# Forgetting attention: probabilities and values split in two, three fp32r passes for one fp32 product

## The chip, the cores and the metric

One core of one Trainium2 chip (trn2) runs the whole program. The metric is the device time of one execution, in microseconds (us). Three runs of the kernel before gave 3176.74, 3176.81 and 3177.16 us; their median is 3176.81. The clock of TensorE has two levels, 1.2 and 2.4 GHz; the profile gives the granted share of the upper one.

## The reference, cut to what matters

A decoder trunk of two layers over 1024 tokens of width 1024: a retention layer and a forgetting-attention layer, each with an MLP. The attention has 16 heads of width 64 and reads keys, values and a cumulative forget gate `f`:

```
logits = q k^T * scale + f[query] - f[key]      (causal, query block against all keys before it)
p = softmax(logits)                             per query row
y = p @ v                                       then sigmoid(og) * y, then @ w_out
```

All is fp32, and the kernel keeps about fp32 precision on TensorE, which has a fast format, fp32r (a rounded fp32), and a slow one, full fp32.

## The kernel before, in words

Projections and the MLP split each operand into a rounded fp32r part ("high") and the rest ("low") and add three fp32r products; ScalarE rounds (`prep`, L646, into `w_hi`), VectorE subtracts (L988, into `w_lo`).

In attention, queries and keys are split the same way and stacked, high and low, on 128 partitions, together with the forget gate in `a2`, `b2`. Probabilities and values are not: `values` (L1887) is a full fp32 product.

For each head `h` of the loop at L1913, TensorE does three things, interleaved by block `n` of twelve (`fox_blocks`: key block against up to 512 queries; in order, 512, 384, 256, 128, 512, 512, 128, 512, 256, 512, 384, 512 columns, 4608 in all):

- `logits(h, n + 1)`: keys by queries, two fp32r passes (L1881, L1882) and for blocks on the diagonal a mask (L1884), into one of two banks;
- `score_tile(h + 1, t)`, queries by keys, for the row maxima of the **next** head (L1857, L1859): eight tiles of 1024 down to 128 columns, in two alternating pairs of banks. A tile waits until the tile two before it was read. `tiles_at` says at which block each stands: at blocks 0 to 6, in heads 0 and 8 at blocks 3 to 8;
- `values(h, n)`: 64 value columns and 64 columns of ones by the probabilities of block `n` (L1902), so that the sum of the probabilities comes out beside the result. It waits for the exponential.

ScalarE takes the exponential of each block of logits (`exps`, L932) into `probs`, and the reciprocal of the sums as Ln and Exp (`inverse_sum`, L941, L943). `z_high` (L949) rounds the gated result of a pair of heads for the out projection.

VectorE takes the maximum of each score tile (`row_max`, L1372), splits the eight columns of maxima in two (`split_max`, L1379, L1381); TensorE transposes them (`max_transpose`, L1868), VectorE copies the rows (`copy_max`, L1385), SP writes them by two DMAs into `a2` of the next head (`save_max`, L435), and `logits(h + 1, 0)` waits for those. VectorE also multiplies the result by the reciprocal and by the gate (`y_gate`, L1395, L1399) and takes the low part of a pair (`z_low`, L1405).

GpSimd issues all other loads of the stage: eight DMAs of queries, keys and gates for head `h + 3` (`load_qk`, L589) once the logits of head `h` are done, the values (`load_v`, L595), the output gate of a pair (`load_og`, L598). Its only arithmetic is the sum of squares before a norm (L502). A first head has places of its own in memory (`q_first` and so on).

After heads 7 and 15 follows the out projection of eight heads (L1517, L1520, L1521), which reads `z_hi`, `z_lo` pair by pair.

Of the kernel before, what the change touches and what calls it, by code (L numbers as in the profile page):

```python
# [21 lines left out]
ALU = mybir.AluOpType  # L22
# [7 lines left out]
P = 128  # L30
# [67 lines left out]
def build(nc, x, vec_a, vec_b, forget_bias, positions, w_ada, kv_w_ada, w_mlp_in, w_mlp_out, ret_w_in,  # L98
          ret_w_out, kv_w, fox_w_in, fox_w_out, ret_decay, out):
    with ExitStack() as ctx:  # L100
# [18 lines left out]
        ((h_hi, h_lo), (rq, rk, rv, rg, rdec, qdec, rs, k_tok, qd), (q1, k1, q2, k2, fv, fog, row_mask), (out_stage,),  # L119
# [7 lines left out]
             ("fv", [P, 2, 8, P], F32), ("fog", [P, S], F32), ("row_mask", [P, S], BF16)],  # L127
# [3 lines left out]
            _, rq_first, rk_first, rv_first) = region(  # L131
# [6 lines left out]
             ("rv_first", [P, 4, RET_DV], F32)])  # L138
# [3 lines left out]
        (misc,), (q1_first, k1_first) = region(  # L142
            20 * 1024, [("misc", [P, 5, S], F32)], [("q1_first", [P, S], F32R), ("k1_first", [P, S], F32R)])
        low_tiles = sb("low_tiles", [P, 2, S])
# [31 lines left out]
        probs = misc[:, 0:4, :].rearrange("p a (b n) -> p (a b) n", n=HALF)  # L176
        y_fox = misc[:, 4, :]
        fv_first = stage[:, 4, :].rearrange("p (b n) -> p b n", n=P)
        qk_hi = misc[:, 3:5, :].bitcast(F32R)
        log_sum = low_tiles[:, 0, :].rearrange("p (b n) -> p b n", n=HALF)  # L180
        max_rows = low_tiles[0:16, 1, 0:P]
# [39 lines left out]
        def scratch(name, shape):  # L221
# [50 lines left out]
        fox_v_loaded = [sem(f"fox_v_loaded{i}") for i in range(2)]  # L272
        first_qk_loaded, first_v_loaded, first_ones_set, second_qk_loaded = (
            sem("first_qk_loaded"), sem("first_v_loaded"), sem("first_ones_set"), sem("second_qk_loaded"))
# [4 lines left out]
        st_full, exp_done, pv_done = sem("st_full"), sem("exp_done"), sem("pv_done")  # L279
        log_done, inv_done, y_read, y_gated = sem("log_done"), sem("inv_done"), sem("y_read"), sem("y_gated")  # L280
        ones_set, row_mask_set = sem("ones_set"), sem("row_mask_set")
# [30 lines left out]
        def probs_slot(e):  # L312

            return 4 + e % 4 if e < NF else e % 8

        def probs_before(e):

            return e - 4 if e < NF + 4 else e - 8

        def tiles_at(h, n):  # L320

            places = {3: (0,), 4: (1,), 5: (2,), 6: (3,), 7: (4, 5), 8: (6, 7)} if h % 8 == 0 else \
                {0: (0,), 1: (1,), 2: (2,), 3: (3,), 4: (4,), 5: (5,), 6: (6, 7)}
            return places.get(n, ())

        def transpose_at(h):

            return 10 if h % 8 == 0 else 8
# [23 lines left out]
        def _(sp):  # L352
# [74 lines left out]
            with sp.Fori(0, 4) as i:  # L427
                for j in range(2):
                    load_pair(i * 2 + (W_FQ + j), j, in_pair(fox_w_in, i * 512 + 256 * j))
            def save_max(h):  # L430

                sp.wait_ge(s_read, h * 9 + 9)
                for n in range(2):
                    row = fox_tiles(h)[2][68 + n:69 + n, :].bitcast(F32)
                    sp.dma_start(row, max_rows[8 * n:8 * n + 8, :]).then_inc(max_loaded, 16)  # L435
            for g in range(2):
                for j in range(2):
                    load_pair(g * 2 + (W_FOX + j), j, out_pair(fox_w_out, g * 512, j))
                for h in range(9) if g == 0 else range(9, FOX_HEADS):
                    save_max(h)  # L440
                    if h == 0:
                        sp.wait_ge(a_full, A_MLP1)
                        for dst, src in head_parts(1)[:4]:
                            sp.dma_start(dst, src).then_inc(second_qk_loaded, 16)
            mlp_loads(W_MLP1, 1)
# [10 lines left out]
        def _(pool):  # L456
# [129 lines left out]
            def load_qk(h, done, first=0):  # L586

                for dst, src in head_parts(h)[first:]:
                    pool.dma_start(dst, src).then_inc(done, 16)  # L589

            def load_v(h):
                at = h % 2 * 64
                rows = fv_s.rearrange("(b p) n -> p b n", p=P)[:, :, h * 64:h * 64 + 64]
                dst, done = (fv_first, first_v_loaded) if h == 0 else (fv[:, h % 2], fox_v_loaded[h % 2])
                pool.dma_start(dst[:, :, at:at + 64], rows).then_inc(done, 16)  # L595

            def load_og(pr):
                pool.dma_start(fog[:], og_s[pr]).then_inc(og_loaded, 16)  # L598
# [8 lines left out]
            load_qk(0, first_qk_loaded)  # L607
            load_v(0)
            with pool.Fori(0, 2) as i:
                for j in range(4):  # L610
                    spill(j, og_s[bass.ds(i * 4 + j, 1)].rearrange("a p n -> p (a n)"),
                          a_free, i * 4 + (A_OG + j + 1))
            pool.wait_ge(a_full, A_MLP1)
            load_qk(1, fox_qk_loaded[1], 4)
            for j in range(4):
                pool.wait_ge(stage_dma[j], E_OG + 32)
            load_og(0)
            load_v(1)
            load_qk(2, fox_qk_loaded[2])
            load_v(2)  # L620
            load_qk(3, fox_qk_loaded[0])
            for h in range(FOX_HEADS):
                if h and h + 3 < FOX_HEADS:
                    wait_run(st_full, h * NF + NF)
                    load_qk(h + 3, fox_qk_loaded[h % 3])
                if h and h + 2 < FOX_HEADS:
                    wait_run(pv_done, h * NF + NF)
                    load_v(h + 2)
                if h % 2 and h + 1 < FOX_HEADS:
                    wait_run(y_gated, h * 2 + 2)  # L630
                    load_og(h // 2 + 1)
# [4 lines left out]
        def _(act):  # L636
# [289 lines left out]
            def exps(h, n):  # L926
# [3 lines left out]
                if probs_before(e) >= 0:  # L930
                    act.wait_ge(pv_done, probs_before(e) + 1)
                nc.scalar.activation(probs[:, probs_slot(e), 0:w], bank[4 + e % 2][:, 0:w], ACT.Exp).then_inc(exp_done, 1)  # L932

            def inverse_sum(h, n):
# [7 lines left out]
                act.wait_ge(log_done, v + 1)  # L942
                nc.scalar.activation(log_sum[sums, n, :], log_sum[sums, n, :], ACT.Exp, scale=-1.0).then_inc(inv_done, 1)  # L943

            def z_high(pr, n):

                cols = slice(HALF * n, HALF * (n + 1))
                act.wait_ge(y_gated, pr * 4 + n + 3)
                nc.scalar.activation(z_hi[:, pr % 4, cols], y_fox[:, cols], ACT.Copy).then_inc(z_hi_done, 1)  # L949
            for h in range(FOX_HEADS):  # L950
                for n in range(NF):
                    exps(h, n)
                    if n == 0 and h % 8:
                        inverse_sum(h - 1, 1)
                    if n in (4, 5) and h % 2 == 0 and h % 8:
                        z_high(h // 2 - 1, n - 4)
                    if n == 6:
                        inverse_sum(h, 0)
                if h % 8 == 7:
                    g = h // 8  # L960
                    inverse_sum(h, 1)
                    z_high(h // 2, 0)
# [13 lines left out]
        def _(dve):  # L976
# [410 lines left out]
            def y_gate(h, n):  # L1387
# [3 lines left out]
                v = h * 2 + n  # L1391
                dve.wait_ge(inv_done, v + 1)
# [3 lines left out]
                if h % 2 == 0 and n == 0:  # L1396
                    dve.wait_ge(og_loaded, h * 8 + 16)
                dve.wait_ge(y_read, v + 1)
                TT(y_fox[mine, cols], y_fox[mine, cols], fog[mine, cols], ALU.mult).then_inc(y_gated, 1)  # L1399
# [9 lines left out]
            nc.vector.memset(fv_first[:, :, 64:128], 1.0).then_inc(first_ones_set, 1)  # L1409
# [10 lines left out]
            nc.vector.memset(fv[:, 1, :, 0:64], 1.0).then_inc(ones_set, 1)  # L1420
            nc.vector.memset(fv[:, 0, :, 64:128], 1.0).then_inc(ones_set, 1)
# [4 lines left out]
            def next_max(h, tiles):  # L1426
                if h + 1 < FOX_HEADS:
                    for t in tiles:
                        row_max(h + 1, t)
            for h in range(FOX_HEADS):  # L1430
                if h % 8 == 0:
                    next_max(h, (0, 1))
                    y_gate(h, 0)
                    next_max(h, (2, 3, 4, 5, 6, 7))
                else:
                    next_max(h, (0, 1))
                    y_gate(h - 1, 1)
                    next_max(h, (2, 3, 4))
                    if h % 2 == 0:
# [553 lines left out]
```

## Time and profile before

| | |
|---|---|
| Median of 3 runs | 3176.81 us |
| The profiled execution's own time | 3181.35 us |
| Its span, first to last instruction | 3179.8 us |
| Mean granted clock of TensorE | 0.991 |
| Busy share of the span: TensorE, VectorE, ScalarE, GpSimd | 98%, 41%, 27%, 7% |
| Attention heads 0 to 7, then 8 to 15 | 2062 to 2223 us, 2267 to 2417 us |

The busy time is that of records whose ends are modelled for TensorE, so what a pass costs is read from the start of one to the start of the next. GpSimd's busy time has its DMA issues in it where they show.

### The profile page before, as it was taken

To read this page: it belongs to the slowest core of one execution; us is meant where nothing else is said; L and a number is where in the kernel's file an instruction comes from. 1 tells how busy PE (TensorE), PEld (TensorE's weight loads), DVE (VectorE), ACT (ScalarE), POOL (GpSimd) and SP (SyncE) were. 2 spreads that over 40 slices of the span, in tenths; PEclk is the share of its full clock that TensorE was granted. 3 is DMA by queue.
4 is the path that set the end of the run, shared out by engine and by line. 5 is a ranking of instruction groups with operands and counts; after the bars stand their busy time and mean duration, and the time that the engine had idled before them with its cause. 6 is when DMAs were issued, how large, how long until landed. Compare 5 with 4: busy or idle time off the path is not lost.

```text
span 3179.8 us, 34523 instructions
## 1 busy us (share of the span) xinstructions
PE 3121.0 (98%) x13726; PEld 2491.4 (78%) x13726; DVE 1308.1 (41%) x1542; ACT 859.3 (27%) x1025; POOL 222.8 (7%) x343
## 2 busy tenths in 40 slices
PE   7999999999999999999999999989999999999999
PEld 4788888877778888888887777756767788888887
DVE  5664323255555333333353243145454533333323
ACT  4111222222242111111134344234244211111112
POOL 0000010000010000000010001023021000000000
PEclk8999999999999999999999999999999999999999
DMA  5555565433201111111112324255241111111111
GB/s 219 189 191 199 176 221 203 174 111 110 97 27 40 53 53 42 50 53 40 54 40 104 109 87 155 96 126 125 65 109 50 40 53 53 40 53 53 40 53 54
DMA packets 144652, 302.50 MB, mean 95 GB/s; under 512 B 10241, under 2 KB 72116, under 8 KB 144564
## 3 DMA queue, kind: packets, MB, share of 16 engines
q1 hardware_dynamic: 111204, 185.90, 17.8%
q0 software_dynamic: 33360, 115.38, 11.7%
q8 instruction: 61, 1.00, 0.1%
q14 instruction: 27, 0.22, 0.0%
HBM read 245.93 MB, written 55.18 MB: 95 GB/s over the span
## 4 chain that ended last, share of the span: by engine, by line
PE 91%; DVE 4%; ACT 2%; DMA 2%; issue 1%; POOL 0%; SPq 0%; DVEq 0%; ACTq 0%; POOLq 0%
PE ps L1521 10%; PE ps L1517 10%; PE ps L1520 10%; PE ps L1478 8%; PE ps L1481 8%; PE ps L1484 8%; PE ps L1634 5%; PE ps L1640 5%; PE ps L1637 5%; PE ps L1902 3%; PE ps L1608 3%; PE ps L1611 3%; PE ps L1612 3%; PE ps L1758 1%; PE ps L1730 1%; PE ps L1857 1%
## 5 line engine op out<-in xcount | busy, mean ns | idle before, releaser
L1517 PE MATMUL ps<-z_hi,w_hi 128*128 128x512 f32 x1408 | 552.0, 392 | 0.0
L1521 PE MATMUL ps<-z_hi,w_lo 128*128 128x512 f32 x1408 | 548.0, 389 | 0.0
L1520 PE MATMUL ps<-z_lo,w_hi 128*128 128x512 f32 x1408 | 547.8, 389 | 0.0
L1478 PE MATMUL ps<-h_hi,w_hi 128*128 128x512 f32 x1152 | 452.0, 392 | 3.9 <-DVE w_lo L988 3.9
L1481 PE MATMUL ps<-h_lo,w_hi 128*128 128x512 f32 x1152 | 449.0, 390 | 0.0
L1146 DVE SCALAR_TENSOR_TENSOR xT<-ps,ada,xT 128x512 f32<-128x512 f32 x352 | 258.8, 749 | 443.3 <-PE ps L1521 443.3
L646 ACT ACTIVATE w_hi<-w_raw 128x2048 fp32r<-128x2048 f32 x116 | 221.4, 1909 | 738.7 <-PE ps L1517 487.7
L988 DVE TENSOR_TENSOR w_lo<-w_raw,w_hi 128x2048 fp32r<-128x2048 f32 x116 | 265.7, 2290 | 246.1 <-ACT w_hi L646 246.1
L1484 PE MATMUL ps<-h_hi,w_lo 128*128 128x512 f32 x1152 | 355.1, 389 | 0.0
L1634 PE MATMUL ps<-h_hi,w_hi 128*128 128x512 f32 x768 | 305.1, 397 | 9.1 <-DVE xT L1146 5.5
L1520 PEld LDWEIGHTS ps<-z_lo,w_hi 128*128 128x128 f32 x1408 | 264.3, 188 | 56.7 <-issue 2.2
L1517 PEld LDWEIGHTS ps<-z_hi,w_hi 128*128 128x128 f32 x1408 | 264.3, 188 | 56.6 <-issue 2.2
L1521 PEld LDWEIGHTS ps<-z_hi,w_lo 128*128 128x128 f32 x1408 | 264.3, 188 | 55.1
L1637 PE MATMUL ps<-h_hi,w_lo 128*128 128x512 f32 x768 | 302.1, 393 | 0.0
L1298 DVE TENSOR_TENSOR misc<-misc 128x1024 f32<-128x1024 f32 x64 | 78.3, 1223 | 452.9 <-ACT misc L834 452.9
L1478 PEld LDWEIGHTS ps<-h_hi,w_hi 128*128 128x128 f32 x1152 | 216.7, 188 | 50.7 <-DVE w_lo L988 3.5
L1481 PEld LDWEIGHTS ps<-h_lo,w_hi 128*128 128x128 f32 x1152 | 216.7, 188 | 45.8 <-issue 1.2
L1484 PEld LDWEIGHTS ps<-h_hi,w_lo 128*128 128x128 f32 x1152 | 216.5, 188 | 45.4
L1640 PE MATMUL ps<-h_lo,w_hi 128*128 128x512 f32 x768 | 251.7, 394 | 0.4 <-DVE h_lo L1030 0.4
L834 ACT ACTIVATE misc<-ps 128x1024 f32<-128x1024 f32 x64 | 65.8, 1028 | 498.8 <-PE ps L1484 250.8
L1634 PEld LDWEIGHTS ps<-h_hi,w_hi 128*128 128x128 f32 x768 | 146.3, 190 | 42.8 <-DVE xT L1146 6.3
L1640 PEld LDWEIGHTS ps<-h_lo,w_hi 128*128 128x128 f32 x768 | 146.3, 190 | 32.3 <-DVE h_lo L1030 1.4
(261 smaller groups left out, 3612.2 us busy)
## 6 DMA issues: line engine op xcount, KB each, us to landing
misc<-w_ada SPq DMA_DIRECT2D x80, 512.0 KB, 5.1
w_raw<-w_mlp_in SPq DMA_DIRECT2D x32, 1024.0 KB, 5.5
w_raw<-w_mlp_out SPq DMA_DIRECT2D x32, 1024.0 KB, 5.0
w_raw<-ret_w_in SPq DMA_DIRECT2D x24, 1024.0 KB, 7.8
qk_s<-stage POOLq DMA_DIRECT2D x16, 512.0 KB, 4.0
v_s<-stage POOLq DMA_DIRECT2D x16, 512.0 KB, 3.6
g_s<-stage POOLq DMA_DIRECT2D x16, 512.0 KB, 3.9
misc<-kv_w_ada SPq DMA_DIRECT2D x16, 512.0 KB, 5.5
```

The costliest lines, as they stand in the source:

```text
L646: nc.scalar.activation(w_hi[:, slot, :], w_raw[:, slot, :], ACT.Copy).then_inc(hi_done, 1)
L988: TT(w_lo[:, slot, :], w_raw[:, slot, :], w_hi[:, slot, :].bitcast(F32), ALU.subtract)\
L1146: STT(out=x_half, in0=bank[ring[q % 4]], scalar=ada[:, gate + q % 8:gate + q % 8 + 1], in1=x_half, op0=ALU.mult, op1=ALU.add).then_inc(d_f ...
L1478: m = MM(outs[hf], hi, b_hi[:, k, cols], start=first, stop=False)
L1481: MM(outs[hf], hi, b_lo[:, k, cols], start=False, stop=False)
L1484: m = MM(outs[hf], lo, b_hi[:, k, cols], start=False, stop=last)
L1517: mm = MM(out_bank, hi, z_hi[:, k, half(hf)], start=k == 0, stop=False)
L1520: MM(out_bank, hi, z_lo[:, k, half(hf)], start=False, stop=False)
L1521: mm = MM(out_bank, lo, z_hi[:, k, half(hf)], start=False, stop=k == 3)
L1634: m = MM(outs[u][hf], w[u][0], h_hi[:, k, half(hf)], start=k == 0, stop=False)
L1637: MM(outs[u][hf], w[u][1], h_hi[:, k, half(hf)], start=False, stop=False)
L1640: m = MM(outs[u][hf], w[u][0], h_lo[:, k, half(hf)], start=False, stop=k == KT - 1)
```

## The change

Probabilities and values are each split into a rounded part and a rest, and `values` becomes three fp32r passes: high values by high probabilities, low by high, high by low.

- Probabilities. ScalarE takes the exponential twice, once into the fp32r tile `probs_hi` and once into `probs`; for blocks 7, 9 and 11 VectorE copies `probs` to `probs_hi` in place of the first. The rest, `probs - probs_hi`, goes to `probs_lo`: on VectorE for blocks 5, 7, 9, 11 (and for the whole of head 0), on GpSimd for the others. `probs_hi` and `probs_lo` lie in slot 1 of `w_hi` and `w_lo`. Each of the tiles has four slots (before, `probs` had eight).
- Values. GpSimd loads them raw, copies them to fp32r (`v_high`) and subtracts (`v_low`); the low parts have zeros where the high ones have the ones.
- TensorE's order: `logits(n + 1)`, score tiles, the two high passes of block `n`, the low pass of block `n - 1`, then the transpose, now at block 7 (in heads 0 and 8 still 10). The low pass of block 11 stands behind the next head's first logits.
- `load_qk` and `load_og` move from GpSimd's queue to SP's, behind `save_max`, for head `h + 2`.
- `y_gate` is parted: `y_scale` for each head, `gate` for a pair of heads at once on 128 partitions. `inverse_sum` is parted in two on ScalarE.
- VectorE's order is written out block by block.

The diff, cut to its core:

```diff
-            return 10 if h % 8 == 0 else 8
+            return 10 if h % 8 == 0 else 7
...
+        HI_ON_DVE = (7, 9, 11)
+        LO_ON_DVE = (5, 7, 9, 11)
+        def low_part(engine, h, n):
+            e, w = h * NF + n, fox_blocks[n][3]
+            engine.wait_ge(exp_done, e + 1)
+            engine.wait_ge(*hi_ready(e))
+            if e >= 4:
+                engine.wait_ge(pv_done, e - 3)
+            engine.tensor_tensor(probs_lo[:, e % 4, 0:w], probs[:, e % 4, 0:w], probs_hi[:, e % 4, 0:w].bitcast(F32),
+                                 ALU.subtract).then_inc(lo_ready(e)[0], 1)
...
 SP, for each head
+                    elif h + 2 < FOX_HEADS:
+                        if h > 1:
+                            sp.wait_ge(st_full, h * NF)
+                        load_qk(h + 2, fox_qk_loaded[(h + 2) % 3])
+                    if h and h % 2 == 0:
+                        sp.wait_ge(y_gated, h)
+                        load_og(h // 2)
...
 GpSimd
-            for h in range(FOX_HEADS):
-                if h and h + 3 < FOX_HEADS:
-                    wait_run(st_full, h * NF + NF)
-                    load_qk(h + 3, fox_qk_loaded[h % 3])
...
+            for h in range(1, FOX_HEADS):
+                for n in (0, 1, 2, 3):
+                    low_part(nc.gpsimd, h, n)
+                if h + 1 < FOX_HEADS:
+                    v_high(h + 1)
+                low_part(nc.gpsimd, h, 4)
+                if h + 1 < FOX_HEADS:
+                    v_low(h + 1)
+                for n in (6, 8, 10):
+                    low_part(nc.gpsimd, h, n)
+                if h + 2 < FOX_HEADS:
                     load_v(h + 2)
...
 ScalarE, exps
+                if e >= 4:
+                    act.wait_ge(*lo_ready(e - 4))
+                if not hi_on_dve(e):
+                    if e >= 4:
+                        act.wait_ge(pv_hi_done, e - 3)
+                    nc.scalar.activation(probs_hi[:, e % 4, 0:w], bank[4 + e % 2][:, 0:w], ACT.Exp).then_inc(p_hi_act, 1)
+                nc.scalar.activation(probs[:, e % 4, 0:w], bank[4 + e % 2][:, 0:w], ACT.Exp).then_inc(exp_done, 1)
...
 VectorE
+            def high_part(h, n):
+                e, w = h * NF + n, fox_blocks[n][3]
+                dve.wait_ge(exp_done, e + 1)
+                if e >= 4:
+                    dve.wait_ge(pv_hi_done, e - 3)
+                    dve.wait_ge(*lo_ready(e - 4))
+                nc.vector.tensor_copy(probs_hi[:, e % 4, 0:w], probs[:, e % 4, 0:w]).then_inc(p_hi_dve, 1)
...
+                for n in range(NF):
+                    if hi_on_dve(h * NF + n):
+                        high_part(h, n)
+                    if lo_on_dve(h * NF + n):
+                        low_part(nc.vector, h, n)
+                    if h + 1 < FOX_HEADS:
+                        for t in tiles_at(h, n):
+                            row_max(h + 1, t)
+                        if n == (8 if h % 8 == 0 else 6):
+                            split_max(h + 1)
+                        if n == transpose_at(h):
+                            copy_max(h + 1)
+                    if h % 8 and n == 1:
+                        y_scale(h - 1, 1)
+                        if h % 2 == 0:
+                            gate(h // 2 - 1, 1)
+                    if h % 2 == 0 and h % 8 and n in (4, 6):
+                        z_low(h // 2 - 1, n // 2 - 2)
+                    if n == 8:
+                        y_scale(h, 0)
+                        if h % 2:
+                            gate(h // 2, 0)
...
 TensorE
-                MM(bank[6 + hf][:, HALF - w:HALF], keys, probs[:, probs_slot(e), 0:w],
-                   start=b == 0, stop=n in (HF0 - 1, NF - 1)).then_inc(pv_done, 1)
+                dst = bank[6 + hf][:, HALF - w:HALF]
+                MM(dst, high[:, b, :], probs_hi[:, e % 4, 0:w], start=b == 0, stop=False)
+                MM(dst, low[:, b, :], probs_hi[:, e % 4, 0:w], start=False, stop=False).then_inc(pv_hi_done, 1)
+            def values_low(h, n):
+                pe.wait_ge(*lo_ready(e))
+                MM(bank[6 + hf][:, HALF - w:HALF], fox_values(h)[0][:, b, :], probs_lo[:, e % 4, 0:w], start=False,
+                   stop=n in (HF0 - 1, NF - 1)).then_inc(pv_done, 1)
...
                 logits(h, 0)
+                if h % 8:
+                    values_low(h - 1, NF - 1)
                 for n in range(NF):
                     if n + 1 < NF:
                         logits(h, n + 1)
                     if h + 1 < FOX_HEADS:
                         for t in tiles_at(h, n):
                             score_tile(h + 1, t)
-                    values(h, n)
+                    values_high(h, n)
+                    if n:
+                        values_low(h, n - 1)
```

## Rows read from the trace of the kernel before

**Rows 1.** The page, the chain that ended last, by engine.

```profile
PE 91%; DVE 4%; ACT 2%; DMA 2%; issue 1%; POOL 0%; SPq 0%; DVEq 0%; ACTq 0%; POOLq 0%
```

**Rows 2.** Stretches: us, PE, PEld, DVE, ACT, POOL busy (x count), clock, DMA.

```profile
2080.00:2100.00 20.00, 15.41 (x60) 9.58 (x59) 7.03 (x20) 5.82 (x11) 1.25 (x3) 0.91 0.55 114
...
2280.00:2300.00 20.00, 16.73 (x60) 10.81 (x61) 6.57 (x18) 4.97 (x10) 5.06 (x9) 0.83 0.45 95
```

**Rows 3.** The transpose of the maxima (L1868), its starts in steady heads.

```profile
L1868 PE MATMUL ps<-ident,max_split x7: 277/277/278, 2109.7 to 2218.9; 128*16 128x128 f32 x7
```

**Rows 4.** Stretches: two steady heads, and head 15.

```profile
2164.38:2200.68 36.30, 36.20 (x162) 23.93 (x162) 20.39 (x48) 17.28 (x34) 10.61 (x19) 1.00 0.54 119
2401.74:2416.80 15.06, 14.35 (x59) 8.46 (x57) 2.75 (x4) 8.00 (x16) 0.00 (x0) 1.00 0.21 65
```

**Rows 5.** Order of time in a steady head: start us, us, engine, line.

```profile
2161.75 0.28 PE L1857 MATMUL ps<-k,q 128*128 128x256 f32 x1
...
2161.95 0.60 ACT L932 ACTIVATE misc<-ps 128x512 f32<-128x512 f32 x1 [0.18 <-PE ps L1882]
...
2162.05 0.27 PE L1859 MATMUL ps<-k,q 68*128 68x128 f32 x1
2162.16 0.43 PE L1902 MATMUL ps<-misc,fv 128*128 128x128 f32 x2
...
2162.74 1.08 PE L1902 MATMUL ps<-misc,fv 128*128 128x512 f32 x2
...
2163.90 0.39 PE L1882 MATMUL ps<-q,k 70*128 70x512 f32 x1
...
2164.16 0.17 DVE L1381 TENSOR_TENSOR max_split<-neg_max,max_split 128x8 f32<-128x8 f32 x1
...
2164.38 0.28 PE L1868 MATMUL ps<-ident,max_split 128*16 128x128 f32 x1
```

**Rows 6.** Order of time in the out projection, two passes of 512.

```profile
2264.02 0.39 PE L1517 MATMUL ps<-z_hi,w_hi 128*128 128x512 f32 x1
...
2264.25 0.39 PE L1520 MATMUL ps<-z_lo,w_hi 128*128 128x512 f32 x1
```

**Rows 7.** Groups by form: busy us, mean ns of one, idle before.

```profile
L932 ACT ACTIVATE misc<-ps 128x512 f32<-128x512 f32 x96 | 57.3, 597 | 117.2 <-PE ps L1882 59.9 <-PE ps L1884 57.2
...
L1405 DVE TENSOR_TENSOR z_lo<-misc,z_hi 128x512 fp32r<-128x512 f32 x16 | 10.4, 686 | 0.1
...
L1379 DVE CAST max_split<-neg_max 128x8 fp32r<-128x8 f32 x16 | 2.7, 171 | 0.6
...
L1061 DVE CAST misc<-misc 128x1024 f32<-128x1024 int32 x1 | 0.7, 694 | 10.2 <-DMA misc<-positions 10.2
```

**Rows 8.** Order of time in the norm after attention, VectorE and GpSimd.

```profile
2456.03 2.28 DVE L988 TENSOR_TENSOR w_lo<-w_raw,w_hi 128x2048 fp32r<-128x2048 f32 x1
2456.49 2.97 POOL L502 TENSOR_TENSOR low_tiles<-misc 128x512 f32<-128x512 f32 x1 [20.00 <-ACT misc L653]
...
2458.89 1.12 DVE L1023 SCALAR_TENSOR_TENSOR misc<-xT,mod,low_tiles 128x512 f32<-128x512 f32 x1
```

**Rows 9.** GpSimd's sums of squares (L502): ns min/median/max.

```profile
L502 POOL TENSOR_TENSOR low_tiles<-low_tiles,misc x24: 1283/1298/1569, 923.4 to 2465.1; 128x512 f32<-128x512 f32 x24
```

**Rows 10.** Order of time: waits in heads 0, 1, 5 and 9.

```profile
2065.28 1.12 PE L1902 MATMUL ps<-misc,stage 128*128 128x512 f32 x2 [2.01 <-ACT misc L932]
...
2088.89 1.40 SPq L435 DMA_DIRECT2D q<-low_tiles  x2
...
2094.03 0.50 PE L1881 MATMUL ps<-q,k 128*128 128x512 f32 x1 [3.78 <-DMA q<-low_tiles]
...
2165.00 1.30 SPq L435 DMA_DIRECT2D q<-low_tiles  x2
...
2168.22 0.79 PE L1881 MATMUL ps<-q,k 128*128 128x512 f32 x1
...
2289.65 0.79 PE L1881 MATMUL ps<-q,k 128*128 128x512 f32 x1 [3.27 <-DMA q<-low_tiles]
```

More of the change, by code:

```diff
@@ L584, in _, with v_tile, v_high, v_low @@
             spill_heads(fq_hi_s, fq_lo_s, 8)
-            def load_qk(h, done, first=0):
-                for dst, src in head_parts(h)[first:]:
-                    pool.dma_start(dst, src).then_inc(done, 16)
+            def v_tile(h):
+                return v_raw_first if h == 0 else v_raw[:]
             def load_v(h):
-                at = h % 2 * 64
[L593 to L598, printed above, removed]
+                if h > 1:
+                    pool.wait_ge(v_split_done, h)
+                rows = fv_s.rearrange("(b p) n -> p b n", p=P)[:, :, h * 64:h * 64 + 64]
+                pool.dma_start(v_tile(h), rows).then_inc(v_raw_loaded, 16)
+            def v_high(h):
+                at = h % 2 * 64
+                pool.wait_ge(v_raw_loaded, 16 * (h + 1))
+                if h >= 2:
+                    pool.wait_ge(pv_done, (h - 1) * NF)
+                nc.gpsimd.tensor_copy(fox_values(h)[0][:, :, at:at + 64], v_tile(h)).then_inc(v_hi_done, 1)
+            def v_low(h):
+                at = h % 2 * 64
+                high, low = fox_values(h)
+                pool.wait_ge(v_hi_done, h + 1)
+                if h == 1:
+                    pool.wait_ge(zeros_set, 1)
+                if h == 2:
+                    pool.wait_ge(zeros_set, 2)
+                nc.gpsimd.tensor_tensor(low[:, :, at:at + 64], v_tile(h), high[:, :, at:at + 64].bitcast(F32),
+                                        ALU.subtract).then_inc(v_split_done, 1)
             for j in range(4):
@@ L947, in z_high @@
                 cols = slice(HALF * n, HALF * (n + 1))
[L948 removed]
+                act.wait_ge(y_gated, pr * 2 + n + 1)
                 nc.scalar.activation(z_hi[:, pr % 4, cols], y_fox[:, cols], ACT.Copy).then_inc(z_hi_done, 1)
@@ L1424, in _ @@
             dve.wait_ge(row_mask_set, 2)
[L1426 to L1429, printed above, removed]
             for h in range(FOX_HEADS):
[L1431 to L1439, printed above, removed]
-                        z_low(h // 2 - 1, 0)
-                        z_low(h // 2 - 1, 1)
-                    next_max(h, (5,))
-                    y_gate(h, 0)
-                    next_max(h, (6, 7))
-                if h + 1 < FOX_HEADS:
-                    split_max(h + 1)
-                    copy_max(h + 1)
+                if h == 1:
+                    dve.wait_ge(st_full, NF)
+                    nc.vector.memset(fv_low_even[:, :, 64:128].bitcast(F32), 0.0).then_inc(zeros_set, 1)
+                for n in range(NF):
[20 more added lines that the diff above has]
+                            gate(h // 2, 0)
                 if h % 8 == 7:
                     g = h // 8
-                    y_gate(h, 1)
+                    y_scale(h, 1)
+                    gate(h // 2, 1)
                     z_low(h // 2, 0)
```

158 lines of the change are left out of this document (96 added, 62 removed).

## The prediction

> **What bounds the kernel now.** I read the page's chain first: TensorE holds 91% of it [rows 1]. Only one stage changes, the sixteen attention heads (the loop at L1913, 2062 to 2417 us), so the rest was read there. The table by stretches shows a granted clock of 0.91 and 0.83 around the starts of heads 1 and 9, each after a wait [rows 2]. The transpose of the maxima runs once a head and paces it: seven of them from 2109.7 to 2218.9, 109.2 / 6 = 18.2 us apart [rows 3]. Over two such heads (36.3 us) TensorE is busy for 36.2, VectorE for 20.4, ScalarE for 17.3, GpSimd for 10.6 (all DMA issues) [rows 4]. So in 13 steady heads (1 to 7, 9 to 14) TensorE's own work is the bound. Heads 0 and 8 end in a wait for the row of maxima; head 15 has no score tiles.
>
> **TensorE's part.** In the order of time, the values of a block of 512 and the first logits pass after them take 2162.74 to 2163.90, 1.16 us [rows 5]. A pass of 512 in fp32r starts 0.23 after the one before it (2264.02, 2264.25 [rows 6]). So one block of 512 of fp32 values costs 0.92. A head has 4608 columns of them: six blocks of 512, two each of 384, 256 and 128. Before, in proportion: 6 x 0.92 + 2 x (0.69 + 0.46 + 0.23) = 8.3 us. After, three passes a block: 18 x 0.23 = 4.1, and 6 x (0.18 + 0.12 + 0.10) = 2.4, since narrow passes cost more than their columns (a pass of 128 takes 0.11, from 2162.05 to 2162.16 [rows 5]): 6.5. That takes 1.8 us a head off TensorE. The transpose's wait for VectorE, 0.25 (2163.90 + 0.23 to 2164.38), is covered by other work after. 18.2 - 1.8 - 0.25 = 16.1.
> On the page "FP8 and Floating Point Precision" (TensorE Precision Notes) the Trainium skill has true FP32 as four passes. By that alone a quarter of 8.3, 2.1 us a head, would go, not 1.8; rows 5 bear out the four.
>
> **What is added.** ScalarE: a second exponential, into `probs_hi`, for nine of twelve blocks: 3 x 0.60 + 2 x (0.49 + 0.38 + 0.28) = 4.1 us (L932; 384 and 256 in proportion [rows 7]). From 8.6 us a head [rows 4] to 12.7. VectorE: four subtractions of 512 at 0.69, as L1405, and three copies of 512. No row shows such a copy; its bounds are 0.17 (L1379, 8 columns) and 0.69 (L1061, 1024 columns) [rows 7]; in proportion, 0.43. That is 4.1 us. Gating a pair at once gives back 0.7. From 10.2 to 13.6, and some 0.04 a hand-off. GpSimd: subtractions of 2560 columns; L502 takes 1.28 us at 512 [rows 9], so 6.4, plus `v_low` 1.3 and `v_high` (0.5 to 1.3; 0.7, nearer a copy than a subtraction). It loses eight DMA issues, which go to SP, where two row transfers a head stand. Behind SP's new waits (`st_full`, `y_gated`) stand loads with most of a head to spare and the next `save_max`, whose data come later than both. No engine's sum reaches 16.1, so the order of the waits decides.
>
> **The chain in the second half of a head.** TensorE to ScalarE takes 0.20 (the next pass takes over at 2161.75, the exponential starts at 2161.95), VectorE to TensorE 0.05 (2164.16 + 0.17 to 2164.38) [rows 5]; I take 0.05 from ScalarE too. By hand, in program order, with these durations: up to block 5 TensorE waits only in even heads, 0.3, for maximum 2 behind `gate`; GpSimd's low parts come 0.7 to 1.2 us early. Then:
> (a) Score tile 7 needs maximum 5, which stands behind `low_part` 5 on VectorE. Begun at once, nothing waits.
> (b) High pass 7 needs maximum 7 (0.45), the split (0.35), in even heads `z_low` (0.69), and copy 7 (0.43): 0.7 us odd, 1.0 even.
> (c) High pass 9 needs copy 9, behind `copy_max`, `y_scale` and in odd heads `gate` (0.28 + 0.69 + 0.69): 0.9 odd, 0.4 even.
> (d) High pass 11 needs exponential 11 (0.60), copy 11 (0.43) and hand-offs, 1.3 us; TensorE has 0.55 of work beside it: 0.75.
> Odd 2.35, even 2.45: with 16.1 that is 18.5. The 2 us saved come back as waits for VectorE.
>
> **The shared resource.** In the norm after attention, GpSimd's L502 began at 2456.49 inside VectorE's L988, which ended at 2458.31, and took 2.97 us: 1.15 after L988's end. VectorE's L1023 of 2458.89 took 1.12, to 0.55 after that GpSimd op's end at 2459.46 [rows 8]. So ops of the two with both inputs in SBUF exclude each other. In the changed head, GpSimd runs `low_part` 4 and `v_low`, 2.6 us in a row, just when `low_part` 5 comes up on VectorE, by my walk 0.2 us after `v_low` began. Blocked, it is 1.1 late: (a) becomes 0.75 in odd heads and, with `z_low` caught too, 1.3 in even ones, so the head takes 19.5. The order hangs on 0.2 us, less than my walk can tell, so I take the middle, 19.0. Thirteen heads: 13 x (19.0 - 18.2) = +10.4. Bounds: -27 (16.1, no wait) and +23 (20.0, the later ones caught too).
> By the Trainium skill, "SBUF — State Buffer", section "SBUF: two separate sides", the port pair is an exclusive lock for the whole instruction, against VectorE ops with two SBUF inputs and its 2-port modes. Rows 8 agree for the first; for copies no row shows it. By that rule the sum would be the second rival's.
>
> **The edges.** Head 1's logits wait 3.8 us for the row of maxima, issued at 2088.89 and there at 2094.03, 5.1 us, while GpSimd's loads for heads 2 and 3 are under way; in a steady head 3.2 is enough (2165.00 to 2168.22). Head 9's wait 3.3, with eight loads issued beside the row [rows 10]. After, those loads stand behind the row on SP: 1.9 and 1.3 less. The wait falls below 2 us, like the one of 2.0 at 2065.28, after which passes kept their length [rows 10], so the half clock goes too: 0.91 and 0.83 over 20 us are 3.6 and 6.8 us at the lower of its two levels, 1.8 and 3.3 us lost [rows 2]. Head 0's own saving goes to VectorE, which has all its subtractions: 0; head 8 saves about 1. So -3.7 and -5.6; bounds of both together 0 (another wait in its place) and -13. Head 15: 15.1 us now [rows 4]; after, ScalarE's 11.5 with (c) and (d): 13.3, -1.8. At the ends of heads 7 and 15 the added low pass waits 0.1, and projection steps of three other pairs cover the rest: 0. The first head's split and the memsets lie under its DMA wait: 0, or 1 us if not. Edges: -11.1.
>
> **Sum.** +10.4 - 11.1 = -0.7 against this execution's own 3181.35 us; the median of the runs lies 4.5 lower: 3176.8 - 0.7, 3176 in round figures. A measurement of this kernel can tell about 0.2% from no change, 6.4 us.
>
> **Rivals.**
> *TensorE stays the bound.* The walk may be slow: back-to-back ops start 0.1 before the one ahead ends, and half of (b) to (d) would go: 17.3 us a head, 13 x -0.9 - 11.1 = -23, 3154; without any wait 3139. For it: VectorE's sum leaves 2.5 us free. Against: (d) is a bare chain. Chance 0.30.
> *The lock decides* (slower): at `low_part` 5, `z_low` and copies and subtractions 7 to 11, against GpSimd's 4, 6, 8, 10 and `v_low`. Beyond 19.0 us a head the change loses; at 19.5 to 20.2 it is +17 to +26 less 11.1: 3183 to 3192, middle 3188. For it: rows 8. Against: GpSimd's late ops are narrow. Chance 0.20.
> *The row waits anyway*: SP late, or slowed as before; both heads stay at half clock, +8, 3184. Chance 0.06.
> *Passes don't get cheap*: three weight loads a block don't hide, the 1.8 us are not saved: +10 or more, 3190. The projection's passes, each with its load at 0.23 [rows 6], speak against. Chance 0.06.
>
> **How the numbers follow.** The likeliest, waits for VectorE that eat the saving, has 0.38, range 3166 to 3186: 0.09 below 3170.4, 0.25 within, 0.04 above 3183.2. Faster 0.30 + 0.09 = 0.39. Same 0.25 + 0.02 (lock) + 0.03 (row) + 0.01 (passes) = 0.31. Slower 0.04 + 0.18 + 0.03 + 0.05 = 0.30. The range 3148 to 3200 reaches past half-gone waits and takes in the lock with edges that pay only half.
>
> **What would show it.** Passes of values 0.23 apart; transposes 18.5 to 19.5 us apart; TensorE's waits put down to VectorE's copies (blocks 7, 9, 11) and to the maximum of tile 5; subtractions on VectorE above 1 us beside GpSimd's; clock 1.00 after heads 0 and 8. Transposes below 17.5 apart, or waits put down to GpSimd's low parts, would prove the walk wrong.

## The result, and the profile after

The changed kernel takes 3208.99 us (median of 4 runs, 3206.89 to 3210.04), the kernel before 3176.98 us beside it (3176.74 to 3179.32): a ratio of 1.0097, 95% interval [1.0084, 1.0110]. It is slower by 32 us. The forecast of 3176 missed, and so did its range, which ended at 3200.

The profiled executions span 3208.5 us after and 3179.8 us before, so the 28.7 us between them are what the traces can place. The transpose of the maxima (now L1974) paces the heads as before [rows 3]. Its starts in the order of time on TensorE (start, us, engine, line):

```profile
2151.05 0.27 PE L1974 MATMUL ps<-ident,max_split 128*16 128x128 f32 x1
...
2172.64 0.41 PE L1974 MATMUL ps<-ident,max_split 128*16 128x128 f32 x1
...
2192.03 0.27 PE L1974 MATMUL ps<-ident,max_split 128*16 128x128 f32 x1
...
2213.64 0.41 PE L1974 MATMUL ps<-ident,max_split 128*16 128x128 f32 x1
```

They are 21.6, 19.4 and 21.6 us apart, where they were 18.2 apart. I call the step that holds blocks 0 to 7 of head h (and blocks 8 to 11 of the head before it) "head h": odd heads take 19.4, even ones 21.6 (heads 2 and 3, 21.1 and 19.2). The 28.7 us divide so (after less before; a transpose has the number of the head whose maxima it turns): the first transpose comes 0.9 later; step 0 to 1, +2.9; 1 to 2, -2.8; the six steps 2 to 8, +13.0; 8 to 9, +3.1; 9 to 10, -2.5; the five steps 10 to 15, +12.6; from there to the end, +1.5. The eleven steady steps make +25.6, nearly all of it. Four of the other terms also hold a moved block: the transpose stands one block earlier than before, but not in heads 0 and 8, so the steps 1 to 2 and 9 to 10 hold one block less than before, and 8 to 9 and the stretch behind the last transpose one more. Such a block (number 8) takes 1.0 us in after (2151.05 to 2152.10), and 1.9 at the lower clock behind the last transpose.

Stretches of after (us, busy of PE, PEld, DVE, ACT, POOL, clock, DMA): heads 2 and 3, heads 5 and 6, four microseconds in each of heads 2 and 6 around block 7, and the starts of heads 1 and 9, to set beside [rows 2, 4]:

```profile
2110.74:2151.05 40.31, 35.16 (x189) 27.58 (x188) 29.70 (x61) 23.25 (x52) 20.71 (x23) 1.00 0.49 108
2172.64:2213.64 41.00, 36.43 (x188) 28.74 (x187) 29.44 (x60) 23.25 (x52) 20.70 (x22) 0.96 0.48 105
...
2130.00:2134.00 4.00, 2.77 (x16) 2.11 (x15) 3.70 (x9) 1.73 (x5) 0.74 (x1) 1.00 0.01 1
2212.00:2216.00 4.00, 3.48 (x12) 2.84 (x12) 2.89 (x6) 0.83 (x2) 0.74 (x1) 0.57 0.01 1
...
2080.00:2100.00 20.00, 16.88 (x72) 12.17 (x71) 11.90 (x30) 8.23 (x18) 2.28 (x2) 0.83 0.45 97
2300.00:2320.00 20.00, 17.77 (x80) 13.61 (x79) 11.04 (x22) 8.96 (x20) 8.90 (x10) 0.83 0.42 95
```

TensorE is no longer its own bound: 36.4 us busy of 41.0, with a clock of 0.96, where it had 36.2 of 36.3 [rows 4]. No other engine is full either (VectorE 29.4). So the order of waits decides. The largest waits of TensorE in the heads, 2040 to 2460 us (line, waited for: us in total, times, longest):

```profile
PE ps L2011 <- DVE w_hi L1497: 28.4, 41, 1.1
PE ps L1963 <- DVE neg_max L1459: 6.3, 13, 0.8
PE ps L1963 <- DMA k<-fk_hi_s: 6.2, 1, 6.2
PE ps L2011 <- ACT w_hi L1008: 3.1, 4, 2.0
PE ps L1987 <- DMA q<-mean_head: 2.6, 2, 1.3
```

L2011 is the high pass, L1497 the copy that rounds the probabilities of blocks 7, 9 and 11 on VectorE: 41 waits of about 0.7 us. L1963 is a score tile, L1459 the row maximum that frees its buffer. An even head shows how they come about (order of time: start, us, engine, line, [idle before <- released by]):

```profile
2206.99 1.29 POOL L669 TENSOR_TENSOR fv_low_odd<-v_raw,fv 128x512 fp32r<-128x512 f32 x1
...
2207.53 1.29 DVE L1503 TENSOR_TENSOR z_lo<-misc,z_hi 128x512 fp32r<-128x512 f32 x1
...
2208.75 0.94 DVE L346 TENSOR_TENSOR w_lo<-misc,w_hi 128x512 fp32r<-128x512 f32 x1
...
2210.28 0.33 PE L1963 MATMUL ps<-k,q 128*128 128x128 f32 x1 [0.78 <-DVE neg_max L1459]
...
2212.04 0.42 DVE L1497 CAST w_hi<-misc 128x512 fp32r<-128x512 f32 x1
...
2212.51 0.80 PE L2011 MATMUL ps<-w_hi,fv 128*128 128x512 f32 x1 [0.98 <-DVE w_hi L1497]
2213.11 0.63 PE L2012 MATMUL ps<-w_hi,fv_low_even 128*128 128x512 f32 x1
2213.54 0.31 PE L2019 MATMUL ps<-w_lo,fv 128*128 128x128 f32 x1
```

While GpSimd subtracts (L669, `v_low`), VectorE's `z_low` takes 1.29 us for its 0.69, `low_part` 5 comes late behind it, so maximum 5, and tile 7 waits 0.78 for that. Then the high pass of block 7 waits 0.98 for its copy. `low_part` 5 takes 1.61 to 1.62 in the odd heads, where `v_low` catches it itself, and copy 11 0.62 us for its 0.43 (0.77 in head 2): it begins while GpSimd issues the load of the next values (L650, 0.91 us from 2155.10) and ends 0.22 after that (2155.61 to 2156.23). Behind the two waits of this even head the granted clock is 0.57: L2012 starts 0.60 after L2011 and L2019 0.43 after that, in place of 0.34 and 0.24 in head 2. The passes are as slow up to 2215.6, so the next step runs slow as well. The even heads 4, 6, 10, 12 and 14 all have such a stretch, of 0.66 over 5 us behind block 7. Head 2 has not: the same two waits, 0.76 and 0.98 us, stand in it at 2128.98 and 2131.21, and the clock stayed at 1.00.

### The profile page after: what moved, and what is told of

Read it like the earlier page. It is cut to its first block and busy times, and to the rows that moved or that the text cites. A ratio compares the mean times of both kernels' runs of the same rounds, so it can differ in the third digit from the quotient of the medians.

```text
span 3208.5 us, 35519 instructions
## 1 busy us (share of the span) xinstructions
PE 3117.1 (97%) x13918; PEld 2525.7 (79%) x13918; DVE 1381.8 (43%) x1649; ACT 907.0 (28%) x1169; POOL 302.6 (9%) x371
```

## The experiments

Each kernel was timed beside the kernel before. Three theories stood against one another at the start. **L**: the exclusion of the two-input operations of GpSimd and VectorE makes the loss. **Q**: VectorE's own queue is enough. **C**: the half clock in even heads is part of it, and follows its waits. "Odd" and "even" are us of a steady head by the starts of the transposes, as most of them take it (head 7 of e3 took 20.6, head 4 of e8 18.4). "Copies" are the three of blocks 7, 9 and 11 on VectorE.

| | edit to the changed kernel | us, median | ratio to before, interval | odd | even |
|---|---|---|---|---|---|
| before | | 3177 to 3179 | | 18.1 | 18.3 |
| after | none | 3209.0 | 1.0097 [1.0084, 1.0110] | 19.4 | 21.6 |
| e1 | `v_low` late | 3193.8 | 1.0052 [1.0035, 1.0069] | 18.9 | 20.3 |
| e2 | `z_low` late | 3198.7 | 1.0064 [1.0047, 1.0081] | 19.7 | 19.7 |
| e3 | both late | 3208.4 | 1.0094 [1.0077, 1.0111] | 22.1 | 19.5 |
| e4 | before, loads on SP | 3173.8 | 0.9987 [0.9978, 0.9997] | 18.1 | 18.3 |
| e5 | no copies | 3173.2 | 0.9981 [0.9972, 0.9991] | 17.4 | 18.2 |
| e6 | no copies, `v_low` late | 3164.6 | 0.9958 [0.9941, 0.9974] | 17.2 | 17.6 |
| e7 | no low parts | 3185.3 | 1.0026 [1.0016, 1.0036] | 18.3 | 19.6 |
| e8 | no copies, low parts all on VectorE | 3179.9 | 1.0006 [0.9997, 1.0016] | 18.1 | 19.4 |
| e9 | no low parts, no copies | 3157.7 | 0.9938 [0.9921, 0.9954] | 17.1 | 17.1 |
| e10 | e6, head 1's loads from two queues | 3165.7 | 0.9964 [0.9952, 0.9975] | 17.1 | 17.6 |
| e11 | no low parts on GpSimd | 3187.7 | 1.0029 [1.0016, 1.0042] | 18.3 | 19.8 |
| e12 | e3 without copies | 3165.3 | 0.9963 [0.9949, 0.9977] | 17.5 | 17.5 |

**e1, the split of the values late.**

```diff
-                if h + 1 < FOX_HEADS:
-                    v_high(h + 1)
-                low_part(nc.gpsimd, h, 4)
-                if h + 1 < FOX_HEADS:
-                    v_low(h + 1)
-                for n in (6, 8, 10):
+                for n in (4, 6, 8, 10):
                     low_part(nc.gpsimd, h, n)
+                if h + 1 < FOX_HEADS:
+                    v_high(h + 1)
+                    v_low(h + 1)
```

> The changed kernel with one move: GpSimd's v_high and v_low for the next head stand behind its low_part 10 instead of around low_part 4. Theory L (the exclusion of two-input operations of GpSimd and VectorE makes the loss): in the changed kernel low_part 5 on VectorE took 1.61 us beside v_low and z_low 1.29; both go back to 0.69, tile 7 no longer waits, heads with odd numbers go from 19.4 to about 18.7 us, heads with even ones from 21.6 to 19.5 to 20.5, the whole about 12 to 18 us faster than the changed kernel (3192 to 3197). Theory Q (the order on VectorE alone, with z_low, split and copy 7 in a row): the waits move by less than 0.3 us a head, gain under 4 us.

15 us came back, the clock is 1.00 in two steady heads (2165 to 2204), and even heads fell by 1.3. So the collision in the middle of the head costs, and the half clock goes with it. The collision itself only moved: `v_low` now stands beside `low_part` 11, which takes 1.60 us, and TensorE waits 0.25 a head for that, where tile 7 had waited 0.78 in even heads and 0.24 in odd ones.

**e2, z_low late**: called at `n in (8, 10)` in place of `(4, 6)`.

> The changed kernel with one move: VectorE's two z_low of a pair stand at blocks 8 and 10 instead of 4 and 6. Theory Q: only even heads change, the copy of block 7 comes 1.3 us earlier, the wait that ends in half clock (21.6 us against 19.4) goes, even heads reach about 19.5: 6 heads x 2.1 = 12 us faster than the changed kernel, 3196. Theory L: low_part 5 is still caught by v_low, even heads stay above 20, gain 5 to 8 us. [...]

10 us came back and all heads take the same 19.7, with clock 1.00. That is nearer to Q (3196) than to L (3201 to 3204, with even heads above 20), though `low_part` 5 is still caught (1.61 and 1.28 us). High pass 7 of even heads waits 0.41 for its copy where it waited 0.98. Odd heads have no `z_low`, but the transpose cuts a head at block 7, so the work moved to blocks 8 and 10 lies in the step of the next, odd head; that took 0.3 more and the even one 1.9 less.

**e3, both.**

> The changed kernel with both moves. Theory L and Q together: odd heads 18.7, even heads 18.7, clock 1.00 in all steady heads; 13 heads x 18.7 against 7 x 19.4 + 6 x 21.6 = 265.4, so 22 us faster than the changed kernel: 3187, still 10 us slower than the kernel before, because of the waits for the copies of blocks 9 and 11. If the waits at copies 9 and 11 grow by what is saved ahead of them, only 10 us are gained.

Nothing came back, though each alone had, and neither of the figures expected for it (3187, or 10 us gained) was met. The trace of e3 shows why, in the second half of an even head, which lies in the step of the next, odd one:

```profile
2129.81 1.09 DVE L1501 TENSOR_TENSOR z_lo<-misc,z_hi 128x512 fp32r<-128x512 f32 x1
...
2130.44 1.58 POOL L669 TENSOR_TENSOR fv_low_odd<-v_raw,fv 128x512 fp32r<-128x512 f32 x1
2130.83 1.48 DVE L1495 CAST w_hi<-misc 128x512 fp32r<-128x512 f32 x1
...
2132.36 0.50 PE L2009 MATMUL ps<-w_hi,fv 128*128 128x512 f32 x1 [1.91 <-DVE w_hi L1495]
```

With `z_low` on VectorE at blocks 8 and 10 and `v_low` on GpSimd in the same place, copy 11 falls into `v_low`: it takes 1.48 us for its 0.43 and ends 0.29 after it. TensorE waits 1.91, and its clock from 2132 to 2136 is 0.67. One collision was taken away and another made.

**e4, the edges alone.** The kernel before with its DMA issues for queries, keys and gates moved to SP as in the change; values stay on GpSimd, probabilities in fp32.

> The kernel before with one part of the change: the loads of queries, keys and the output gate go from GpSimd's queue to SP's, behind the row of maxima; probabilities and values stay fp32. My step on the edges: head 9 and head 1 get their row in 3.2 us after its issue and keep the full clock, 4 to 9 us faster than before, 3168 to 3173. Rival: head 1's first score tile waits longer for its keys, since SP issues them one after another at 0.6 us (in the changed kernel that wait was 6.2 us against 4.0): 1 to 3 us of it are given back, 3172 to 3176.

By its starts the step 1 to 2 fell from 21.4 to 17.2 and 9 to 10 from 22.4 to 17.2 (-4.2 and -5.2; the prediction had -3.7 and -5.6), with clock 1.00 in both places. But step 0 to 1 grew by 3.5: head 1's first tile waits 7.9 us for its keys where it waited 4.0. With 3173.8 the rival's range (3172 to 3176) holds, and mine (3168 to 3173) just does not. The trace is of the fastest of the ten executions, 3169.2, so the clock of 1.00 in both places may not be in all of them.

**e5 and e6, no copies.** The same edit of one line in both, e6 with that of e1 as well:

```diff
-        HI_ON_DVE = (7, 9, 11)
+        HI_ON_DVE = ()
```

> The rounded probabilities of blocks 7, 9 and 11 of each head are written by a second exponential on ScalarE (as for the other nine blocks) and not by a copy on VectorE. In the trace of after, TensorE waits 28.4 us in all (41 times) for that copy. ScalarE is busy for 11.6 us of an average head, so three more exponentials of 0.60 us fit. Theory L (the exclusion of the two-input operations of GpSimd and VectorE makes those copies late; with no copy only blocks 9 and 11's rounded part is in time, and what is left is the third pass and the tile's maximum): the waits of the second kind go and odd heads fall from 19.4 us to about 17.4, even ones from 21.6 to about 18.5: 3209 - 14 x 2.5 = about 3174. Theory Q (VectorE's queue as a whole is the bound, 14.8 us of operations a head plus what they wait for one another): only the 1.3 us a head of the copies comes back, and the waits move to the low parts and the maxima: 3209 - 18 = about 3190.

> As the last one, and GpSimd splits the next head's values after its last low part, as in e1_vlow_late (which gave 3194 where after gave 3209). Theory L: with no copy on VectorE at block 11, the late split of the values has only row maxima and low part 11 to hold up, so the gain of both adds: odd and even heads near 17.4 us, about 3168. Theory Q: 3186 to 3190, as the last. If the late split delays low part 11 (third pass of block 11, then the next head's first), heads stay at 18 to 18.5: about 3180.

e5 gives back 36 us and e6 44, by which e6 beats both kernels: 13 us under before. The waits for VectorE's copies are gone. In e5 the largest that is left in steady heads is the one collision that theory L names, in even heads:

```profile
2193.31 1.73 POOL L669 TENSOR_TENSOR fv_low_odd<-v_raw,fv 128x512 fp32r<-128x512 f32 x1
...
2193.82 1.77 DVE L346 TENSOR_TENSOR w_lo<-misc,w_hi 128x512 fp32r<-128x512 f32 x1
...
2196.18 0.33 PE L1963 MATMUL ps<-k,q 128*128 128x128 f32 x1 [1.25 <-DVE neg_max L1459]
```

e6 takes it away too. The waits of TensorE in e6 from 2100 to 2220, nearly seven heads, are these three and no more:

```profile
PE ps L2017 <- POOL w_lo L346: 0.4, 1, 0.4
PE ps L2017 <- DVE w_lo L346: 0.3, 1, 0.3
PE ps L2009 <- ACT w_hi L1006: 0.2, 1, 0.2
```

e5 met L's figure (3174); Q's 3190 for it is out. e6 came 3 us under its own (3168). But L's reason, that the exclusion makes the copies late, is not what e5 shows: e7, next, has the same waits for copies without any of them stretched. The figure was right by luck.

**e7 and e9, no low parts.** The third pass reads the rounded part; e7 keeps the copies, e9 does not.

> Left out: every low part of the probabilities, on both engines; the third pass reads the rounded part instead, so that TensorE still runs its three passes; buffers are released by the values' end. It tells what TensorE's own work of a head comes to when no subtraction stands beside it. The prediction had 16.1 us a head for it (18.2 before). If that was right, heads come at 16.1 to 16.5 us, but for what the copies of blocks 7, 9 and 11 cost: theory L expects nearly nothing of them without the exclusion (16.5 to 17.0 a head, about 3209 - 14 x 3.8 = 3156). If the three passes are not as cheap as three plain ones (theory P), heads come at over 17.3 with hardly a wait on TensorE: 3165 or more.

> Left out: every low part of the probabilities (the third pass reads the rounded part, as in e7_no_low_parts), and the rounded parts of blocks 7, 9 and 11 are written on ScalarE. So neither copies nor subtractions stand on VectorE, and TensorE should be its own bound: this measures the term of the prediction that had 16.1 us a head. Theory R (the term was right): 16.1 to 16.3 us a head, even and odd alike. Theory M (mis-sized: the rows of e6 give 6.97 us a head for the three passes where the prediction took 6.5): 16.5 to 16.9 a head, about 3157 less than e6's 17.1 to 17.9 allow: 3150 to 3158.

e7 missed by 29 us. Without a single low part, on either engine, heads still take 18.3 and 19.6: each of its three copies a head takes 0.43 and none was stretched, but TensorE waits 28.2 us in all for them (46 times), as much as in after. The copies cost by their place in VectorE's queue, with no help of the exclusion; theory P, which had hardly a wait on TensorE, is out as well. e9 then gives TensorE's own work: 17.1 a head, even and odd alike, where the prediction had 16.1. Its time, 3157.7, is at the upper end of what theory M gave (3150 to 3158), its heads are above M's 16.5 to 16.9. Its passes, in the order of time on TensorE:

```profile
2156.49 0.23 PE L1979 MATMUL ps<-ident_b,mask_b 128*128 128x128 bf16 x1
2156.53 0.42 PE L2000 MATMUL ps<-w_hi,fv 128*128 128x384 f32 x1
2156.79 0.34 PE L2001 MATMUL ps<-w_hi,fv_low_even 128*128 128x384 f32 x1
2156.97 0.39 PE L2008 MATMUL ps<-w_hi,fv 128*128 128x512 f32 x1
2157.41 0.50 PE L2000 MATMUL ps<-w_hi,fv 128*128 128x512 f32 x1
```

A pass of 384 takes 0.18 (2156.79 to 2156.97), but 0.26 when it is the first behind the bf16 pass of the mask (2156.53 to 2156.79). The next step, 0.44 for a pass of 512 that takes 0.23, is a wait of 0.21 for ScalarE's exponential of block 11.

**e8, every low part on VectorE**, no copies; GpSimd only splits the values.

> Rounded parts all on ScalarE (as e5), and all twelve low parts of a head on VectorE; GpSimd only splits the values, at the start of a head. VectorE is then busy for 14.8 - 1.3 + 8 low parts x 0.65 us = 18.7 us a head by its durations in after, but those hold some that were stretched by the exclusion (1.61 for 0.69). Theory L: without stretching, VectorE needs about 16.5 to 17 a head and TensorE waits for it at the tiles' maxima: 17.5 to 18.2 a head, 3170 to 3180. Theory Q: the longer queue on VectorE makes it worse than after: 19.5 to 21 a head, 3195 to 3215.

3179.9 is the upper end of L's range, and odd heads (18.1) are as L had them; even ones (19.4) are between the two theories. It is 7 us worse than e5. VectorE is busy for 31.1 us of two heads (36.5). Sharing the subtractions with GpSimd pays once the copies are gone.

**e10, two queues for head 1.** e6, with the last four loads of head 1 issued by GpSimd.

```diff
-                        load_qk(1, fox_qk_loaded[1], 4)
 ...
+            load_rest(1, second_rest_loaded)
             load_v(1)
```

> e6_hi_scalar_vlow_late (3164.6, head 0 took 38.3 us by the transposes, head 1's first tile waited 5.2 us for its keys) with the last four loads of head 1 issued by GpSimd again, beside SP's first four. Theory S (the edges' loss in head 0 is the eight loads of head 1 in one queue, one after the other; in the kernel before they went out from two): the wait falls from 5.2 us to about 4.0 and head 0 by 1.2 to 2.5 us: about 3162.5. Rival (the wait is the transfers themselves, with those of head 2 and the weights beside them): no change in head 0, 3164.5.

Step 0 to 1 fell from 38.3 to 37.0 us, as S expected, and the wait from 5.2 to 3.0, but step 9 to 10 took 1.5 more than in e6, at a clock of 0.90 for 1.00, and the time is the same (3165.7 for 3164.6, where S had 3162.5). The eight loads in one queue explain a part of the growth in head 0; one trace of each kernel shows it, and whether it can be turned into time stays open.

**e11, no low parts on GpSimd.** VectorE keeps copies and low parts 5, 7, 9 and 11; the other blocks' third pass reads the rounded part.

> Left out: the low parts that GpSimd makes (blocks 0 to 4, 6, 8 and 10 from head 1 on); their third pass reads the rounded part. GpSimd splits the next head's values at the head's start. VectorE keeps all that it has in after: copies 7, 9 and 11 and low parts 5, 7, 9 and 11. Theory L (the exclusion alone costs what is above the bare chain): odd heads from 19.4 us to about 18.5, even from 21.6 to about 19.7, with clock 1.00: after's 3209 - 14 x 1.4 = about 3189, close to the 3185 of e7. Theory Q (VectorE's own queue, with four low parts more than in e7): 19.2 to 20.5 a head, 3198 or more.

3187.7, as L expected, with the heads within 0.2 of e7's. So VectorE's own four low parts cost 2 us. The other 21 up to after are not the price of GpSimd's low parts alone, since this edit also takes `v_low` away from `low_part` 5: e1, which moves `v_low` and keeps them all, gives 15 of the 21 back, so some 6 are left for them. VectorE's low parts here and in after (L346: ns min/median/max), first e11:

```profile
L346 DVE TENSOR_TENSOR w_lo<-misc,w_hi x72: 289/691/696, 2064.5 to 2424.3; 128x512 fp32r<-128x512 f32 x66, 128x384 fp32r<-128x384 f32 x2, 128x256 fp32r<-128x256 f32 x2, 128x128 fp32r<-128x128 f32 x2
```

and after:

```profile
L346 DVE TENSOR_TENSOR w_lo<-misc,w_hi x72: 290/693/1616, 2066.7 to 2446.3; 128x512 fp32r<-128x512 f32 x66, 128x384 fp32r<-128x384 f32 x2, 128x256 fp32r<-128x256 f32 x2, 128x128 fp32r<-128x128 f32 x2
```

Alone none takes over 0.70 us; beside GpSimd's the longest takes 1.62.

**e12, e3 without copies.**

> e3_both_late (3208.4; in every second head the copy of block 11 took 1.48 us beside GpSimd's subtraction of the values, TensorE waited 1.9 us for it and its clock fell) with the rounded parts of blocks 7, 9 and 11 on ScalarE. Theory L (that copy was what fell to the exclusion): no wait of over 1 us is left, the clock stays at 1.00, and the time is that of e6, 3160 to 3170. Theory Z (the late low part of z on VectorE is what holds TensorE up, whoever writes the rounded part): every second head stays above 19 us: 3185 or more.

43 us under e3 for the same one line as in e5, and 3165 as L expected. What fell to the exclusion in e3 was the copy, and with it the clock.

## Why the prediction was wrong, point by point

**TensorE's own work: mis-sized.** "18.2 - 1.8 - 0.25 = 16.1" is 17.1 in e9. The fp32 values before were sized right: from start to start over four heads, values and first logits pass take 10.5 us a head, the logits pass alone (from e9) 2.2, so 8.3 are left, as in the prediction. Three passes came to 7.4 in e9, not 6.5: the first pass behind a bf16 pass of the mask takes 0.08 more, four times a head; 0.2 is the wait for the exponential of block 11; the rest is spread (with these two a pass of 512 takes 0.27 in the mean where the shortest take 0.23). And the transpose's wait of 0.25 went, but one of 0.12 or 0.26 came at high pass 8, for its exponential. Thirteen heads of 1.0 us are 13 us off all that the change could bring. So of the 8.3 neither the 1.8 of the rows went nor the 2.1 of a full quarter, but 0.9.

**The chain (a) to (d): right in kind, somewhat long.** The waits stand where the walk put them: in after, copies 7, 9 and 11 of an odd head cost 0.41, 0.87 and 0.69 where the prediction had 0.7, 0.9 and 0.75, copy 7 of an even one 0.98 for 1.0, and tile 7 waits for maximum 5. e11 has the copies without GpSimd's low parts: its waits for them come to 1.2 and 2.4 us in two steps, 1.8 a head, against the walk's 2.4, and its head to 19.1 in the mean, against 18.5. The walk's waits were 0.6 too long and the work under them 1.0 too short; the two errors partly hid each other.

**The shared resource: the choice that failed.** The prediction had 18.5 without and 19.5 with the lock and "took the middle, 19.0". The lock is there in odd and even heads: `low_part` 5 takes 1.61 us beside `v_low` in odd heads, `z_low` 1.29 in even ones. Between e11 and after the mean head grows by 1.4 (19.1 to 20.5), where the middle gave it 0.5. Heads 2 and 3 of after tell the lock from the clock, since they ran at 1.00: 21.1 and 19.2 against e11's 19.8 and 18.3, 1.1 a head. So the lock costs 1.1, the whole 1.0 between the prediction's two cases. Some 0.3 of it is copy 11 beside GpSimd's DMA issue, which the prediction had not seen as an operation that locks. The half clock, which no step of the prediction had in a steady head, adds 0.3: the slow passes take some 1.5 us more in every second head (heads 4 and 5 laid beside 2 and 3), but the waits for copies 9 and 11 behind them shrink from 0.25 and 0.85 us (head 3) to none and 0.52 (head 5), so that two heads lose 0.7 by it. Theory C holds to this size, but what sets the clock in a steady head is not these two waits alone, as head 2 has them too; that stays open. With 20.5 against the 19.0 forecast a head is 1.5 longer: 0.6 from the two terms above, 0.6 from the lock, 0.3 from the clock. Eleven steady heads took 25.6 us more than before; thirteen at that rate make +30 where the prediction had +10.4.

**The edges: the waits right, the clock wrong.** Here the step that failed is "The wait falls below 2 us", so "the half clock goes too". In e4 both terms came (-4.2 and -5.2), with waits for the row of 1.2 us and clock 1.00. In after the row of maxima came sooner too: the waits are 1.3 and 1.3 us for 3.8 and 3.3 [rows 10]. But the clock did not come back: 0.83 over 2080 to 2100, where it had been 0.91, and 0.83 over 2300 to 2320, the start of head 9 now, where it had been 0.83 [rows 2]. Waits for copies of 1.1 and 0.7 us now stand ahead of the row's in both heads 0 and 8. What decides the clock there stays open: in e11 the waits for the row are 1.28 and 1.29 and the steps have 1.00 and 0.82, in e9 both are 2.05 and the steps have 1.00 and 0.82. The steps came to -2.8 and -2.5; each holds a block of 1.0 us less than before and the 1.2 by which an odd head grew, and these cancel.

The other edges went the wrong way. Step 0 to 1 grew by 2.9: head 1's first tile waits 6.2 us for its keys, whose eight loads now leave from one queue, where it waited 4.0, and a wait of 1.1 for a copy came in. Head 8 was to save 1: step 8 to 9 grew by 3.1, 1.0 of it the moved block, and TensorE's waits in it rose from 1.0 to 3.2 us. Head 15 was to save 1.8: from its first logits pass to the out projection it takes 16.6 us (2430.85 to 2447.41) where it took 15.0. Of the 28.7 us between the traces thirteen heads at the steady rate are +30, so the edges, and whatever differs outside the heads, came to -1.6 where the prediction had -11.1.

**The rivals.** "The lock decides" (3183 to 3192) comes nearest, and the change lost 17 us more than it was given. It is one part of the mechanism: the lock and the clock behind it are some 21 us (after over e11), the copies, caught or not, 28 (e7 over e9). Beyond 19.0 us a head the change loses, it said; the heads took 20.5. "TensorE stays the bound" is what e6 is, at 17.1 to 18.0 a head (the rival had 17.3). By the Trainium skill's "SBUF — State Buffer", section "SBUF: two separate sides", VectorE's 2-port modes are locked out as well as its operations with two SBUF inputs. The prediction left this aside for copies, as no row showed it. A copy is caught indeed: 1.48 us for 0.43 in e3. That it runs in such a mode no run here shows.

**What the parts of the change cost**, by medians: three passes with neither copies nor low parts (e9) take 20 us off before. The copies alone add 28 (e7), VectorE's low parts 2 more (e11), GpSimd's low parts and the place of `v_low` between them 21 more (after), of which the place of `v_low` is 15 (e1). The order matters: without copies all low parts together cost 15 (e5), and with `v_low` out of their way 7 (e6).

## What to carry to other kernels

A rounding copy from one engine's output on another, between producer and TensorE, is a hop on the critical chain. If the producer has room (ScalarE was busy for 11.6 of 20.5 us a head), let it write both forms: here that gave 36 us (e5). Before giving GpSimd subtractions, list which VectorE operations will run beside them, copies included, and move the longest of GpSimd's, not the VectorE ones; moving both can make a new pair. A walk whose answer hangs on 0.2 us should be priced at both ends, not in the middle. And a step that counts on the clock coming back should be priced without it too: the same waits left it at either level.

## What the runs showed of the hardware

- A one-input copy fp32 to fp32r of 128x512 on VectorE takes 0.43 us; beside a GpSimd subtraction it ended 0.29 after GpSimd's end and took 1.48 (e3). Beside a DMA issue of GpSimd it took 0.62 and 0.77 and ended 0.22 and 0.23 after the issue's end (after, 2155.61 and 2135.80).
- VectorE's subtraction of 128x512 with both inputs in SBUF takes 0.69 us alone (at most 0.70 in e11) and up to 1.62 in after, 1.77 in e5, beside a GpSimd subtraction.
- The clock went to its lower level in five of six even heads of after behind waits of 0.78 and 0.98 us, 2 us apart (0.57 over 2212 to 2216). In head 2 the same waits left it at 1.00 (2130 to 2134), and in e11 so did a wait of 0.98 in the same place, without the one before it (2200 to 2204).
- The first fp32r pass behind a bf16 pass starts the next one 0.08 us later than the others of its width.
